# Pick groups and one-hot pairs begin 16 dots earlier in the order of VectorE and GpSimd

## The reference

```python
v1, i1 = lax.top_k(s1, K)
v2, i2 = lax.top_k(s2, K)
cand = (v1[..., :, None] + v2[..., None, :]).reshape(B, L, PH, K * K)
top_s, pos = lax.top_k(cand, K)
idx = jnp.take_along_axis(cidx, pos, axis=-1)
gate = jax.nn.softmax(top_s, axis=-1)
...
u = U[ib]
h = jax.nn.gelu(jnp.einsum('thkd,td->thk', u, xb).astype(jnp.float32), approximate=False)
w = (gb * h).astype(xb.dtype)
return jnp.einsum('thk,thkd->td', w, V[ib])
```

## Time and profile before

| | us |
|---|---|
| median of three executions | 3665.36 |
| the profiled execution | 3664.0 |
| its span in the trace | 3662.3 |
| TensorE busy | 3577.6 (98%) |
| VectorE busy | 2058.6 (56%) |
| GpSimd busy | 976.2 (27%) |
| ScalarE busy | 621.3 (17%) |
| dense U on TensorE | about 1339 to 1728 |
| pick groups, pairs of one-hots, last dots | about 1729 to 1963 |
| remaining one-hots | 1963 to 2020 |
| dense V | 2020 to 2570 |

### The profile page before, as it was taken

One profiled execution on the slowest core, in us unless ns is written; L12 is line 12 of the kernel. 1 busy time (PEld: TensorE's weight loads), 2 busy tenths in 40 slices (PEclk: granted clock), 3 DMA queues, 4 the chain that ended last, 5 costly groups with the idle time before them and its releaser, 6 DMA issues. The chain is left out here.

```text
span 3662.3 us, 51124 instructions
## 1 busy us (share of the span) xinstructions
PE 3577.6 (98%) x20754; PEld 3164.9 (86%) x20754; DVE 2058.6 (56%) x4109; ACT 621.3 (17%) x1423; POOL 976.2 (27%) x813
## 2 busy tenths in 40 slices
PE   8999999999999999999898999999999999999999
PEld 6878887899998888888787777777799999999988
DVE  4883102055540399865698544444466766676653
ACT  0002202100002112221167100000222222222100
POOL 0000100101000156675886555455100112222000
PEclk9999999999999999999999999999999999999999
DMA  5433432344444699999895899999533422221352
GB/s 217 140 137 138 143 134 81 116 161 172 188 184 183 237 333 401 404 409 362 290 349 200 314 336 331 347 335 331 183 139 125 150 99 99 99 99 70 141 197 111
DMA packets 159014, 776.65 MB, mean 212 GB/s; under 512 B 19476, under 2 KB 21420, under 8 KB 122812
## 3 DMA queue, kind: packets, MB, share of 16 engines
q1 hardware_dynamic: 100536, 518.52, 38.8%
q0 software_dynamic: 57344, 251.69, 18.4%
q10 hardware_dynamic: 900, 3.17, 0.3%
HBM read 762.67 MB, written 10.64 MB: 211 GB/s over the span
## 5 line engine op out<-in xcount | busy, mean ns | idle before, releaser
L405 PE MATMUL PS<-mem,ring 128*128 128x272 f32 (+1 forms) x2816 | 645.0, 392 | 3.0 <-DMA ring<-in_first_tiles 3.0
L405 PEld LDWEIGHTS PS<-mem,ring 128*128 128x128 f32 x2816 | 539.7, 192 | 106.1 <-issue 4.6
L1281 POOL DMA_INDIRECT mem<-in_peer_ug,idx x256 | 358.0, 1398 | 535.1 <-DVE idx L1795 346.4
L1933 DVE SCALAR_TENSOR_TENSOR mem<-mem 128x768 f32<-128x768 f32 x256 | 261.3, 1021 | 286.8 <-DMA mem<-in_peer_vg,idx 280.8
L1848 DVE CUSTOM_DVE_ANT_0 mem<-mem 128x1152 f32<-128x1152 f32 x256 | 348.4, 1362 | 96.7 <-DMA mem<-in_peer_ug,idx 96.5
L1395 PE MATMUL PS<-mem 128*128 128x256 f32 x1792 | 387.5, 379 | 1.7 <-DMA mem<-in_peer_ud 1.6
L1395 PEld LDWEIGHTS PS<-mem 128*128 128x128 f32 x1792 | 340.2, 190 | 48.6 <-DMA mem<-in_peer_ud 2.5
L1307 POOL DMA_INDIRECT mem<-in_peer_vg,idx x256 | 281.3, 1099 | 281.4 <-DVE mem L1933 232.1
L413 PEld LDWEIGHTS PS<-mem,ring 128*128 128x128 f32 x3136 | 350.3, 192 | 0.1
L413 PE MATMUL PS<-mem,ring 128*128 128x128 f32 x3136 | 350.3, 275 | 0.0
L2279 PE MATMUL PS<-mem,ring 128*128 128x128 f32 x2560 | 312.3, 275 | 0.9 <-issue 0.6
(11 more groups left out here) (413 smaller groups left out, 4467.0 us busy)
## 6 DMA issues: line engine op xcount, KB each, us to landing
ring<-in_first_tiles SPq DMA_DIRECT2D x144, 1024.0 KB, 4.8
ring<-in_dn_tiles SPq DMA_DIRECT2D x88, 1024.0 KB, 5.3
mem<-in_peer_vd SPq DMA_DIRECT2D x128, 640.0 KB, 6.9
mem<-in_peer_ud SPq DMA_DIRECT2D x128, 448.0 KB, 6.8
ring<-in_out_panels SPq DMA_DIRECT2D x16, 2048.0 KB, 8.3
ring<-in_w_out SPq DMA_DIRECT2D x8, 2048.0 KB, 9.0
ring<-in_peer_wq SPq DMA_DIRECT2D x8, 2048.0 KB, 8.0
mem<-second_keys SPq DMA_DIRECT2D x64, 256.0 KB, 5.2
```

The costliest lines, as they stand in the source:

```text
L405: last = nc.tensor.matmul(PS[:, 4 + n % 4, 0:T if wide else TX], wslots[slot_of[n]][:, k, :], x, start=(k == 0), stop=(k == KT - 1))
L1281: nc.gpsimd.indirect_dma_start(ugs[at % US], None, a["peer_ug"], bass.IndirectOffsetOnAxis(ap=idx[:, n, j:j + 1], axis=0)).then_inc(u_in[a ...
L1933: nc.vector.scalar_tensor_tensor(hc, Vg[:, at % GS, :], dots[:, m, h * PTOP + j:h * PTOP + j + 1], hc, ALU.mult, ALU.add).then_inc(vg_used, 1)
```

## The change

The first unit with pick groups behind it is 11 x 16 = 176 instead of 12 x 16 = 192. PAIR0 is worked out from it, 186 instead of 202, and SPREAD too, 68 units instead of 52. The number of pairs stays 60.

```diff
-        NPG, PICK0, PER, AHEAD = P // 4, 12 * PTOP, 4, 2
+        NPG, PICK0, PER, AHEAD = P // 4, 11 * PTOP, 4, 2
         PAIR0, NPAIR = PICK0 + NPG // PER + AHEAD, 60
         SPREAD = HN * PTOP - 2 - PAIR0
```

## The result

The changed kernel took 3691.73 us (median of four runs, 3687.86 to 3693.02) against 3664.68 us for the kernel before beside it. The ratio is 1.0069 with a 95% interval of 1.0056 to 1.0083, so 21 to 30 us slower. The same kernel timed once more in a later set, beside 26 runs of the kernel before, gave 1.0051 (1.0035 to 1.0066), 13 to 24 us. Both intervals leave out "no change".

A forecast was written before the change was run, and what follows sets the result against it. The prediction took TensorE to bound the program but VectorE the pair stretch, where the moved dots land. 20.5 - 1.6 - 3.0 + 1.5 = +17.4 us, so 3682.8 us against the median of 3665.36; range 3675 to 3691.

The forecast's parts named there:

- The dots behind the gate cost VectorE's own time: Pair stretch (1812 to 1963 us): 16 dots moved behind dense U's end cost 1.28 us each on VectorE, +20.5 us.
- The gate does not move, the stall of 1.61 us goes: End of dense U: picks start no earlier, but TensorE's single wait for a dense U tile goes, -1.6 us, or 0.
- The two waits in front: Before the first picks: VectorE stands about 45 us and GpSimd about 50 us, waiting for dense U's end and second keys.
- The waits for the scatter go: Pair stretch: most of VectorE's 4.5 us of waits for TensorE's scatter go, -3.0 us, between 0 and -4.5.
- New waits: Pair stretch: fuller DMA engines bring new waits for gathers or keys, +1.5 us, bounds 0 and +9.
- Stretched instructions: Pair stretch: about a tenth of VectorE's 11 us of instructions stretched beside GpSimd would go, 1 us; full removal 11 us.
- The early stretch is the same: First 34 pick groups, 1730 to 1812 us: same rhythm of dots and gathers, 0 us, bounds -2 and +2.
- Behind 1963 only the start changes: Last one-hots and dense V: they start later but take as long, and none of the delay is made up.
- The last dot, said to end near 1980: End of the pair stretch: last dot near 1980 us instead of 1963; before 1970 would prove the forecast wrong.
- The DMA engines: Rival, pair stretch: transfers become the pace at share 0.94, +23 to +25 us in all, 3689 to 3691; chance 0.13.
- a floor of 162 us: Pair stretch: 165 us of transfers fit closely into 168 us, share 0.98, against 1.02 to 1.03 reached in dense U.
- TensorE's lower clock: Rival, pair stretch: thinner work drops TensorE's clock to 0.76, its work taking 178 us, +25 us, about 3691; chance 0.05.

The follow-up runs named there:

- e4: The kernel before with 16 dots of the pair stretch done twice on VectorE, no gather or transfer added; 1.0059, +21.6 us.
- e6: The changed kernel with 16 gathers of its pair stretch replaced by plain transfers of 16 columns, dots whole; 1.0048, +17.6 us against the kernel before.
- e5: The changed kernel with 16 dots of its pair stretch over 16 columns instead of 1152, gathers whole; 1.0032, +11.7 us against the kernel before.
- e9: The changed kernel with 16 dots cut to 16 columns and GpSimd's pair-stretch masks over 256 columns instead of 512; 1.0038, +13.9 us against the kernel before.
- 196: The kernel before with unit 196 instead of 192 as the first with pick groups, four more dots before the gate; 0.9998, between -4 and +3 us.
- e10: The changed kernel with only the masks of its pair stretch cut to 256 columns; 1.0031, +11.4 us against the kernel before.

## Why the prediction was right, point by point

**The dots behind the gate cost VectorE's own time (+20.5): right, and shown.** e4 adds 16 dots and no transfer to the kernel before and gives the changed kernel's pair stretch (171.5 and 171.7 us) and its time. e6 leaves the dots and takes the gathers away, and the cost stays.

**The gate does not move, the stall of 1.61 us goes (-1.6): right.** Dense U is 1.3 us shorter, 387.9 against 389.2, and the first pick sum comes 2.0 us behind it as before. The two waits in front were said to be 45 and 50 us and are 45.92 and 50.17.

**The waits for the scatter go (-3.0): right, and more than that.** 4.5 us before, none of them in either trace after. **New waits (+1.5): right in size.** The wait for a gather went from 1.1 to 2.5 us. VectorE's whole list of waits from 1822 to 1994 in the changed kernel is this, 4.4 us against 7.2 before:

```profile
DVE mem L1848 <- DMA mem<-in_peer_ug,idx: 2.5, 1, 2.5
DVE mem L1835 <- issue: 1.0, 1, 1.0
DVE mem L1848 <- ACT mem L1595: 0.9, 1, 0.9
```

**Stretched instructions (1 us of gain named, left out of the sum): no gain.** VectorE's own work there is 70 dots of 1.28 us, 120 one-hots of 0.26 and 124 pick sums of 0.27, 154 us; with the waits that leaves 13 us of 171.7. The same count for the whole stretch before (54 dots, 120 one-hots, 124 pick sums, 134 us, waits 7.2) leaves 13 of 154.3 as well. The one-hots became longer and the dots shorter. So +20.5 for dots and -2.8 for waits are 17.7, with 17.4 and 17.6 measured, and 20.5 - 3.0 + 1.5 = 19.0 predicted for this stretch.

**The early stretch is the same (0, between -2 and +2): right within what can be told,** +2.0 as the mean of seven against four.

**Behind 1963 only the start changes: right.** The last one-hots and dense V, 605.6 us before, take 605.8 and 604.2. The last dot, said to end near 1980, ended at 1993.8 and at 1986.5: 7.9 and 2.1 us of that lay before dense U, 6.5 and 4.4 in the early stretch.

**The size.** Forecast +17.4, most likely +13 to +21; the second timing says +18.7, the traces of the second comparison +19.7 with 2.1 of it from before dense U. The first timing says +25.3. That is outside +13 to +21 and at the far end of the range, where the prediction had put its rivals (the median of those four runs lies 0.7 us above the top of 3691). By that number alone the forecast would have been right in its range and not in its size. The excess is not in the pair stretch, which is the same in both traces. It is on both sides: the changed kernel's median was 3.3 us higher than in the second set, and the kernel before's 3.8 us lower. The runs of one kernel go in part by their mean granted clock: the 74 runs of the kernel before in the later sets lie 2.3 us higher per 0.001 less of it, by a straight line through them (correlation -0.65). Against that line the changed kernel's ten runs on record from the first set (mean clock 0.989) are +16.9 us and the five of the second (0.991) +17.4. This is an estimate, and a low one by up to 2 us, since some 0.001 of the changed kernel's lower clock is its own (0.97 instead of 0.99 over 172 us). It suggests that what the first timing had more goes with the clock outside the changed part; what sets the clock from run to run stays open.

**The rivals.** The DMA engines were given 0.13 as the pace, +23 to +25. They are not the pace by themselves, since taking transfers away (e6) wins nothing certain. But they stand close behind, closer than the prediction had them. It gave them a floor of 162 us, by the 1.02 to 1.03 of dense U; in the pair stretches with all gathers they reached 0.96 to 0.98, and without the dots' work those stretches still took 172.0 (e5) and 170.0 us (e9), at a cost of +11.7 and +13.9 us in time. That floor was mis-sized by some 8 to 10 us. The sum of the prediction held all the same, since it took the larger of the two paces and put 1.5 us on it; in the traces the two are equally long, so there was less room than the prediction saw. TensorE's lower clock was there, 0.97 instead of 0.99 in the pair stretch, and no cost of it is seen, TensorE's 144.60 us of work being hidden under VectorE's 170.08; the clock was far from 0.76. The stretched instructions beside GpSimd did not become fewer with a thinner mix: 109 of 120 one-hots began while GpSimd was at work before, 112 of 120 after. That is against what I worked out from the rule of the exclusive port in the Trainium skill (SBUF — State Buffer, "Who interferes with whom"). The rule's kind of blocking is there: halving the masks brought the longest one-hot that began in one from 965 to 547 ns. But it is not for a whole instruction of GpSimd, as the Trainium skill has it: the one-hot of 0.96 us above ended 0.55 us before the mask that it met did. And the prediction left out the gathers that GpSimd issues; one-hots begun in one of those are longer too.

**What was not foreseen** is on the other side: 196 gives nothing that can be told. By the rows of the kernel before, VectorE's 9.29 us and GpSimd's 11.87 us of waiting looked like room for four dots. They were, in the pair stretch of the one trace (-7.2 us); 3.2 us of it were given back in the early stretch, and the timing shows none of the rest.

## What to carry to other kernels

Here work that an engine did while another one was the pace cost nothing; put behind the gate, where its own engine is the pace, it cost its full time, and that is read from two like instructions back to back (here 1.28 us each), less the waits that it fills. Where removing a cost wins little, remove its neighbour as well before saying that it did not matter: dots alone and transfers alone each kept the traced stretch at 170 us or more, and only both gone brought 154. And count two traces from the first changed instruction: here 7.9 of 31.0 us were there before it.

## What the hardware showed that I had not expected

VectorE's one-hot of 128x128 takes 0.34 us by itself (0.26 us from start to start in a row of them), and 413 to 510 ns on the mean of a pair stretch beside GpSimd, in different traces of nearly the same program: the same mix of instructions meets in different ways. Half the masks, another order, fewer or more dots did not settle it, and by the means it is worth up to 12 us of VectorE's time (97 ns times 120). It is not the masks alone: a one-hot that began while GpSimd issued a gather took 407 ns on the mean before and 473 after.

The granted clock between 500 and 750 us, with the same instructions, was 0.96 in some executions and 0.92 in others, and dense U began 8 us later in those.

And the transfers of the pair stretch, gathers in packets of 4608 bytes with keys and memory weights in packets of 2048 beside them, went at 354 to 365 GB/s at a share of 0.96 to 0.98 where the 16 gathers were added (the changed kernel twice, e5, e9, e10), while gathers and dense U tiles (4608 and 3584 bytes) reached 409 at 1.03.
